# Gathered expert rows handled whole: one VectorE instruction of 2048 columns a row, both of its buffers freed together

## The reference, cut to what matters

```python
q = (h @ w_peer_q)...; s = q . peer_keys          # 8 heads, 2 halves, 128 keys each
fv, idx = 16 best of the 16 x 16 sums of the best  # 128 experts a token, out of 16384
g = softmax(fv)
u = peer_u[it]                                     # 128 gathered rows of 2048 a token
act = gelu(einsum('thkd,td->thk', u, xt)) * gt     # a dot product a row
out = einsum('thk,thkd->td', act, peer_v[it])      # a weighted sum of gathered rows
```

## Time and profile before

| | |
|---|---|
| time, median of 3 runs | 3721.91 us (3718.39 to 3725.88) |
| the profiled execution | 3721.31 us, of which its span is 3719.3 us |
| TensorE busy | 3596.1 us, 97% |
| VectorE busy | 2954.6 us, 79% |
| GpSimd busy | 1667.5 us, 45% |
| bytes moved by DMA | 996.32 MB, 268 GB/s on average |

### The profile page before, as it was taken

How to read it: one execution, slowest core, us unless ns; L and a number is a source line. 1 busy time by engine, 2 the same in 40 slices (tenths; PEclk the granted TensorE clock), 3 DMA queues, 4 the chain that set the end, 5 groups by cost and what they waited for, 6 DMA issues and landing times. The chain is left out here.

```text
span 3719.3 us, 61122 instructions
## 1 busy us (share of the span) xinstructions
PE 3596.1 (97%) x22591; PEld 3448.3 (93%) x22591; DVE 2954.6 (79%) x4716; ACT 1428.6 (38%) x1873; POOL 1667.5 (45%) x1357
## 2 busy tenths in 40 slices
PE   8999999999999999999999999999999999999998
PEld 5778778899999999999999999999999999999898
DVE  5482467877778788888888788899989998888877
ACT  3443455566334444343266333333333332332221
POOL 0444432301654554335610455555656555665433
PEclk9999999999999999999999999999999999999999
DMA  6223218887488899843555999999999999998887
GB/s 213 85 85 103 79 51 271 303 305 270 143 316 326 326 327 329 286 142 132 182 189 218 346 351 348 345 345 343 351 340 352 344 333 334 348 355 327 298 320 255
DMA packets 240691, 996.32 MB, mean 268 GB/s; under 512 B 24864, under 2 KB 63848, under 8 KB 187496
## 3 DMA queue, kind: packets, MB, share of 16 engines
q1 hardware_dynamic: 125936, 583.31, 43.3%
q0 software_dynamic: 111152, 404.87, 30.1%
q10 hardware_dynamic: 3464, 6.37, 0.7%
HBM read 960.83 MB, written 33.55 MB: 267 GB/s over the span
## 5 line engine op out<-in xcount | busy, mean ns | idle before, releaser
L909 ACT ACTIVATE w_hi<-ring 128x1024 fp32r<-128x1024 f32 (+1 forms) x499 | 557.0, 1133 | 1030.9 <-DMA ring<-w_exp 861.2
L2149 PE MATMUL bank<-h_hi,w_hi 128*128 128x320 f32 (+1 forms) x2304 | 728.1, 316 | 19.3 <-DVE w_lo L1980 6.9
L877 POOL DMA_INDIRECT grow<-v_rows,g_col x384 | 498.3, 1298 | 529.3 <-DVE g_acc L1792 252.1
L2149 PE MATMUL bank<-h_hi,w_lo 128*128 128x320 f32 (+1 forms) x2304 | 722.1, 313 | 0.0
L2149 PE MATMUL bank<-h_lo,w_hi 128*128 128x320 f32 (+1 forms) x2304 | 719.5, 313 | 0.0
L2149 PE MATMUL bank<-act_hi,w_hi 128*128 128x320 f32 x2048 | 635.8, 310 | 22.7 <-DVE xT L2039 21.8
L2149 PE MATMUL bank<-act_lo,w_hi 128*128 128x320 f32 x2048 | 633.9, 310 | 0.0
L2149 PE MATMUL bank<-act_hi,w_lo 128*128 128x320 f32 x2048 | 633.8, 309 | 0.0
L2022 DVE TENSOR_TENSOR w_lo<-ring,w_hi 128x1024 fp32r<-128x1024 f32 x448 | 545.6, 1218 | 49.1 <-ACT w_hi L909 44.0
L909 ACT ACTIVATE p_hi<-ring 128x512 fp32r<-128x512 f32 x464 | 290.6, 631 | 593.0 <-PE bank L2149 552.8
L2149 PE MATMUL bank<-norm_hi,p_hi 128*128 128x384 f32 (+1 forms) x1216 | 447.0, 368 | 13.5 <-DVE p_lo L1836 10.4
(11 more groups left out here) (330 smaller groups left out, 6839.7 us busy)
## 6 DMA issues: line engine op xcount, KB each, us to landing
ring<-w_exp SPq DMA_DIRECT2D x256, 1024.0 KB
ring<-w_mix SPq DMA_DIRECT2D x107, 1024.0 KB, 6.5
ring<-w_o SPq DMA_DIRECT2D x27, 1024.0 KB, 5.2
ring<-w_pq SPq DMA_DIRECT2D x26, 1024.0 KB, 5.3
a_raw<-w_mix SPq DMA_DIRECT2D x21, 1024.0 KB, 6.3
ring<-w_qk SPq DMA_DIRECT2D x20, 1024.0 KB
tables<-wt SPq DMA_DIRECT2D x10, 2048.0 KB, 6.4
wg<-tables SPq DMA_DIRECT2D x80, 256.0 KB
```

Source lines behind the costliest of these rows:

```text
L877: pool.indirect_dma_start(grow[to][:, :], None, rows, bass.IndirectOffsetOnAxis(g_col[b][:, half:half + 1], 0)).then_inc(gath_in[to], 16)
L909: return nc.scalar.activation(out, in_, func, **kw)
L2149: return nc.tensor.matmul(out, lhsT, rhs, start=start, stop=stop)
```

## The change

Rows with index 104 and up are handled whole: VectorE waits for both halves, runs one `scalar_tensor_tensor` of 2048 columns, and then adds 2 to `gath_free`. The two half buffers of a row become views of one `whole_row` buffer at the same addresses. `half_dot` keeps its two halves for the first 104 rows. The sum of a weighted row now waits until the whole row before has been added (`gath_free` at 2n + 4, where each half waited for 2n + half + 3). The gathers stay as they are: two indirect DMAs of 1024 columns a row, each with its own wait. The partial sums `g_more` are needed for the first 104 rows alone (`N_B` = 104), and `x_more` not at all.

```diff
-        grow = [place(f"grow{i}", row_at[i], [D // 2]) for i in range(4)]
+        whole_row = [place(f"grow{i}", row_at[2 * i], [KC, P]) for i in range(2)]
+        grow = [whole_row[i // 2][:, 8 * (i % 2):8 * (i % 2) + 8, :].rearrange("p a n -> p (a n)") for i in range(4)]
...
-            def a_dot(n, b, tok, sums, i, some=range(2)):
-                for half in some:
-                    row = half_row(n, b, half)
-                    v.scalar_tensor_tensor(out=row, in0=row, scalar=1.0, in1=tok[:, halves[half], :], op0=ALU.mult,
-                                           op1=ALU.mult, accum_out=sums[half][:, bass.ds(i, 1)]).then_inc(gath_free, 1)
+            def row_in(n, b):
+
+                for half in range(2):
+                    dve.wait_ge(gath_in[2 * b + half], 8 * n + 16 - 8 * b)
+                return whole_row[b][:, :, :]
+
+            def a_dot(n, b, tok, sums, i):
+
+                row = row_in(n, b)
+                v.scalar_tensor_tensor(out=row, in0=row, scalar=1.0, in1=tok[:, :, :], op0=ALU.mult, op1=ALU.mult,
+                                       accum_out=sums[:, bass.ds(i, 1)]).then_inc(gath_free, 2)
...
             def an_add(n, b, acc, by, i):
-                for half in range(2):
-                    row, to = half_row(n, b, half), acc[:, halves[half], :]
-                    dve.wait_ge(gath_free, 2 * n + half + 3)
-                    v.scalar_tensor_tensor(out=to, in0=row, scalar=by[:, bass.ds(i, 1)], in1=to, op0=ALU.mult, op1=ALU.add
-                                           ).then_inc(gath_free, 1)
+
+                row, to = row_in(n, b), acc[:, :, :]
+                dve.wait_ge(gath_free, 2 * n + 4)
+                v.scalar_tensor_tensor(out=to, in0=row, scalar=by[:, bass.ds(i, 1)], in1=to, op0=ALU.mult, op1=ALU.add
+                                       ).then_inc(gath_free, 2)
...
-                        v.tensor_tensor(g_dot[:, :], g_dot[:, :], g_more[:, :], ALU.add).then_inc(gath_act, 1)
-                        v.tensor_tensor(x_dot[:, :], x_dot[:, :], x_more[:, :], ALU.add).then_inc(gath_act, 1)
+                        v.tensor_tensor(g_dot[:, 0:N_B], g_dot[:, 0:N_B], g_more[:, 0:N_B], ALU.add).then_inc(gath_act, 2)
```

More of the change, by code:

```diff
@@ L1785, in half_dot @@
+            def a_dot(n, b, tok, sums, i):
+                row = row_in(n, b)
+                v.scalar_tensor_tensor(out=row, in0=row, scalar=1.0, in1=tok[:, :, :], op0=ALU.mult, op1=ALU.mult,
+                                       accum_out=sums[:, bass.ds(i, 1)]).then_inc(gath_free, 2)
             def half_dot(n):
-                a_dot(n // 2, n // 2 % 2, h_tok, (g_dot, g_more), n // 2, (n % 2,))
+                i, half = n // 2, n % 2
+                row = half_row(i, i % 2, half)
+                v.scalar_tensor_tensor(out=row, in0=row, scalar=1.0, in1=h_tok[:, halves[half], :], op0=ALU.mult,
+                                       op1=ALU.mult, accum_out=(g_dot, g_more)[half][:, i:i + 1]).then_inc(gath_free, 1)
@@ L1795, in dot @@
+                v.scalar_tensor_tensor(out=to, in0=row, scalar=by[:, bass.ds(i, 1)], in1=to, op0=ALU.mult, op1=ALU.add
+                                       ).then_inc(gath_free, 2)
             def dot(i, b):
-                a_dot(i, b, h_tok, (g_dot, g_more), i)
+                a_dot(i, b, h_tok, g_dot, i)
             def x_row_dot(i, b):
-                a_dot(i + PAIRS, b, x_tok, (x_dot, x_more), i)
+                a_dot(i + PAIRS, b, x_tok, x_dot, i)
             def gather_add(i, b):
```

## The result

The kernel after takes 3975.17 us (median of 4, 3972.28 to 3979.09) where the kernel before took 3723.89 beside it: a ratio of 1.067, 95% interval 1.0645 to 1.0695. It is slower, as forecast, but by 251 us and not by 30, and outside the range.

What follows compares the result with a forecast made beforehand. TensorE sets the pace, 11.3 us a buffer pair; the gather loop would pass it at 11.57 us. 3721.3 + 32 (120 loops x 0.27) - 2 (tail) = 3751 us, 0.8% slower; range 3719 to 3815.

Steps and rivals of the forecast that it cites:

- the gather loop: Dots and sums: VectorE frees a buffer, GpSimd gathers, DMA lands, VectorE reuses; 9.3 to 11.57 us, costing 32 us; chance 0.60.
- L: Time from a gather's start to the use that waits for it; taken as 6.9 us, ends 6.4 and 8.0.
- my own sum: Changed loop is 4.67 us plus L, 11.57 us; its excess over TensorE's 11.3 us, times 120 loops, gives 32 us.
- my upper end of 168 us: Loss in the full stages with L at 8.0 us, 120 x 1.4; not believed whole.
- The supposed shrinking: At the upper end the DMA engines would be less crowded, which would shorten L.
- the case of 3827: Rival with L = 7.5 us for all rows: loop 12.2 us, 108 us more, 3827 us; chance 0.15.
- The tail: Last 29 rows: shorter VectorE instructions save 4 us, of which 2 us were counted as gain.
- Hidden by the DMA queue: Rival: later gathers only queue less, L shrinks, loop stays near 10.5 us; no change, 3719 us; chance 0.18.
- Faster: Rival: fewer VectorE instructions return TensorE's waits in the tail and at group ends; 3710 us; chance 0.07.
- The two loops feeding each other: Rival: late rows delay remainders and tile loads, TensorE waits on either, L does not shrink; 3827 us; chance 0.15.
- The block of GpSimd by VectorE: A gather's instruction stands still until VectorE's present instruction ends; longer sums hold it up to 1.2 us, one row in five.

Runs made afterwards that it cites:

- the three runs without the long instruction: Kernel before, still 1024-column instructions: both halves given back together, ratio 1.0413; VectorE waiting for both halves first, 1.0177; both parts together, 1.0673.

## Why the prediction was wrong

**The bound was named rightly.** VectorE's 10 to 14% of slack was mostly waiting for rows; the gather loop was the thing to cost, and its excess went to TensorE, whose waits for outputs and remainders between 2040 and 3664 us grew from 33.7 to 183.7 us. Sums of 2.35 us and dots of 2.29, gathers at 3.16 and 4.62 us, waits for rows far above 200 us and nothing lost before 1600 us all came as written; the DMA rate did not, since it fell by 55 GB/s in the sums and not by a few. That the release and the wait each cost time, and together all of it, is shown by the three runs without the long instruction.

**The step that failed is L.** I wrote "I take 6.9", read from the kernel before, and carried it into the kernel after, where I supposed that it would stay or shrink. Measured, the second gather of a row took 9.1 us there to the use that waited (124 of 192 rows). With it my own sum gives 4.62 + 9.1 = 13.7 us a loop, 120 x (13.7 - 11.3) = 288 us: near the 246 us by which the first row of the tail is late (3477.5 us before, 3723.6 after), and far from 32.

As a reading of the kernel before, 6.9 was not bad: the 228 second gathers between 2100 and 3400 us landed there after 6.9 us in the median. But this median covers two clusters, and I had seen both: the 26 landings of the earlier trace rows are all second gathers, eleven with a mean of 6.5 us and fifteen with a mean of 9.2. I did not ask what parts them. By the table above it is a tile's load issued just behind the gather, so L depends on the moment of the issue, and the change moves that moment by 1 us, into the late cluster. So even a careful mean of the kernel before, some 7.2 to 8.1 us, which is at most about my upper end of 168 us, would have been too low.

I also mixed the two gathers of a row. The 7.58 us of the row at 3064.22 is counted from its first gather, 3056.64, while the changed loop waits for the second. The first ones did behave as I supposed when the DMA engines emptied from 94% to 82%: their mean landing fell from 6.7 to 5.5 us. That of the second ones rose from 7.2 to 8.1 us. The supposed shrinking is what I used to set aside the end of 168 us and the case of 3827.

**The tail.** I counted 2 us gained. The windows of the earlier trace rows begin it at 3432 us, which is too early: its 29 rows start between 3477.5 and 3702.2 us before, 224.7 us, and between these in the kernel after:

```profile
3723.59 2.34 DVE L1802 SCALAR_TENSOR_TENSOR x_acc<-grow,x_act,x_acc 128x2048 f32<-128x2048 f32 x1
```

and 3956.0 us, 232.4 us: 7.7 us more. With whole rows in the tail alone they start between 3494.4 and 3727.8 us, 233.3 us, 8.7 more than before. These are single traces, but both point to a small cost and neither to a gain. With one row a tile, a loop of 13.5 us stands against 14, so whatever lands later than usual can go to TensorE; that this is where the 8 us come from is not shown.

**The rivals.** Hidden by the DMA queue: refuted, since L of the second gather grew instead of shrinking. Faster: refuted; it needed L below 6.6. The two loops feeding each other: its size, over 100 us, was nearer than my forecast, and its premise that L does not shrink held for the second gather. Its mechanism did not, since VectorE waited 22.6 us for tiles where it had waited 44.0. The block of GpSimd by VectorE is as the earlier trace rows showed: the copy at 3105.73 took 2.25 us, until about the end of the sum at 3107.94. But as part of the loss it is small, for the run without long instructions lost the same 6.7%.

**What stays open.** Why a load issued behind a gather delays it, beyond that its bytes and its moment count; what a better moment of the tile's load would be worth in time; where the 1.8% of the wait alone arises; and what the last 0.4% of the kernel with one gather is.

## What to carry to other kernels

Where two buffers circle between a consumer, an issuer and a DMA, write the loop down as release, issue, landing, use, for each piece apart, and compare it with the pace of the bound: joining two pieces makes the last release and the last landing count for both. Take the landing time of the piece that will be waited for, and ask what else is issued at the moment to which the change moves it: a landing time read before the change holds only for the old moment. And a merged consumer wants a merged transfer: one gather for the whole row took 1.067 back to 1.004, while merging only the instruction and its waits cost 6.7%.

## What the runs showed of the hardware

TensorE's granted clock fell with its gaps. Before, in the sums from 2640 to 3250 us, TensorE was busy for 605.7 of 610 us and the clock stood at 1.00 of 2.4 GHz:

```profile
2640.00:3250.00 610.00, 605.71 (x4114) 604.66 (x4113) 547.19 (x600) 187.98 (x213) 357.58 (x321) 1.00 0.94 342
```

That is 147 ns of busy time a matmul. After, with waits of up to 9.4 us, the granted clock is 0.94 and 0.95 in the two windows of the result, a mean over times at 2.4 and times at 1.2 GHz, and a matmul of the sums takes 734.42 / 4731 = 155 ns. TensorE's busy time grew by 72 us in all (3596.1 to 3668.2). The gather loop set the pace, so I take this as lying inside it and as no cause of its own; no run tests that apart. A reader who sees only TensorE's busy time rise could take it for one.

GpSimd's gather instruction is held by VectorE. In the trace of the kernel after, 108 of the 111 gathers beside which VectorE ran no two-input instruction took 0.93 to 0.97 us, and 425 of the 431 that began under one ended 0.80 to 0.84 us after its end.
